# Two transformer blocks in one launch: the head of the program is put in another order, with two later moves

## The reference

```python
mod   = silu(c) @ w_ada + b_ada          # 6 x 1024: sh1, sc1, gt1, sh2, sc2, gt2
mod_c = silu(c_ctx) @ w_ada + b_ada
h  = rmsnorm(x, g_norm1) * (1 + sc1) + sh1
hc = rmsnorm(ctx, g_norm1) * (1 + scc1) + shc1
cq, ckv, kpe, rq, rk, rv, rg = split(h @ w_in)      # the same of hc
q = rmsnorm(cq, g_q) @ w_uq ; k, v from rmsnorm(ckv, g_kv) @ w_ukv
```

## Time and profile before

| | us |
|---|---|
| time, median of 3 (860.28 to 862.14) | 860.43 |
| the profiled execution | 860.81 |
| its span | 858.6 |
| PE busy | 832.7 (97%) |
| weight loads (PEld) busy | 719.3 (84%) |
| DVE busy | 587.7 (68%) |
| ACT busy | 469.6 (55%) |

### The profile page before, as it was taken

The page is one execution under the profiler, slowest core; times in us unless marked ns, Lnnn a source line. Parts: engine busy times, 40 slices in busy tenths (PEclk is TensorE's granted clock), DMA queues, the critical chain, the costliest instruction groups (busy, mean ns, idle before and its releaser), DMA issues. The chain is left out here.

```text
span 858.6 us, 12796 instructions
## 1 busy us (share of the span) xinstructions
PE 832.7 (97%) x4917; PEld 719.3 (84%) x4917; DVE 587.7 (68%) x917; ACT 469.6 (55%) x757; POOL 17.7 (2%) x24
## 2 busy tenths in 40 slices
PE   5999999999999999999999999999999999999997
PEld 4788887867899999987889977788977788888785
DVE  4775968797787778897757677577446655555444
ACT  6686355266456655663456674646535645454442
POOL 1001000000000000000000000010000000000000
PEclk9999999999999999999999999999999999999999
DMA  9964473155656666669758543244605566655551
GB/s 332 355 222 124 148 227 130 50 173 162 205 175 210 181 180 184 178 207 307 240 166 285 175 152 116 75 145 152 194 11 163 171 196 182 186 180 188 185 159 49
DMA packets 103507, 152.85 MB, mean 178 GB/s; under 512 B 6506, under 2 KB 55702, under 8 KB 103448
## 3 DMA queue, kind: packets, MB, share of 16 engines
q1 hardware_dynamic: 102136, 149.15, 55.1%
q10 hardware_dynamic: 1312, 2.90, 1.0%
HBM read 150.97 MB, written 1.05 MB: 177 GB/s over the span
## 5 line engine op out<-in xcount | busy, mean ns | idle before, releaser
L2073 DVE TENSOR_TENSOR w_lo<-raw,w_hi 128x1024 fp32r<-128x1024 f32 (+1 forms) x244 | 294.5, 1212 | 159.1 <-ACT w_hi L1510 158.4
L1510 ACT ACTIVATE w_hi<-raw 128x1024 fp32r<-128x1024 f32 (+1 forms) x244 | 254.8, 1051 | 205.5 <-PE bank L737 141.6
L735 PE MATMUL bank<-w_hi,hT_hi 128*128 128x512 f32 (+2 forms) x400 | 156.0, 390 | 1.8 <-DVE w_lo L2073 1.2
L737 PE MATMUL bank<-w_hi,hT_lo 128*128 128x512 f32 (+2 forms) x400 | 152.9, 382 | 0.0
L736 PE MATMUL bank<-w_lo,hT_hi 128*128 128x512 f32 (+2 forms) x400 | 152.6, 382 | 0.0
L839 PE MATMUL bank<-hT_hi,w_hi 128*128 128x256 f32 x512 | 145.0, 283 | 0.0
L840 PE MATMUL bank<-hT_lo,w_hi 128*128 128x256 f32 x512 | 144.9, 283 | 0.0
L841 PE MATMUL bank<-hT_hi,w_lo 128*128 128x256 f32 x512 | 144.9, 283 | 0.0
L840 PEld LDWEIGHTS bank<-hT_lo,w_hi 128*128 128x128 f32 x512 | 98.3, 192 | 0.0
L841 PEld LDWEIGHTS bank<-hT_hi,w_lo 128*128 128x128 f32 x512 | 98.3, 192 | 0.0
L839 PEld LDWEIGHTS bank<-hT_hi,w_hi 128*128 128x128 f32 x512 | 98.3, 192 | 0.0
(11 more groups left out here) (341 smaller groups left out, 1196.3 us busy)
## 6 DMA issues: line engine op xcount, KB each, us to landing
raw<-w_up_dram SPq DMA_DIRECT2D x132, 256.0 KB, 3.3
raw<-w_ada_dram SPq DMA_DIRECT2D x48, 512.0 KB, 4.7
raw<-w_down_dram SPq DMA_DIRECT2D x44, 512.0 KB, 4.4
raw<-w_in_dram SPq DMA_DIRECT2D x40, 512.0 KB, 4.5
raw<-w_gate_dram SPq DMA_DIRECT2D x44, 256.0 KB, 2.9
raw<-w_out_dram SPq DMA_DIRECT2D x16, 512.0 KB, 3.4
raw<-wk_x_dram SPq DMA_DIRECT2D x8, 512.0 KB, 4.5
raw<-wv_x_dram SPq DMA_DIRECT2D x8, 512.0 KB, 3.4
```

The lines of the kernel that those rows point to most:

```text
L735: pe.matmul(o, xh, yh, start=first, stop=False, skip_group_check=skip)
L737: return pe.matmul(o, xl, yh, start=False, stop=last, skip_group_check=skip)
L1510: act.activation(unit_view(w_hi[n % NSPLIT], u), unit_view(raw[u % NRAW], u), ACT.Copy).then_inc(w_hi_ready, 1)
L2073: dve.tensor_tensor(unit_view(w_lo[n % NSPLIT], u), unit_view(raw[u % NRAW], u), unit_view(w_hi[n % NSPLIT], u).bitcast(F32), ALU.subtract ...
```

## The change

The identity is loaded by SP as its first transfer, and only the two small columns and the ones come on ACT's queue (`in_sel`). `x` comes in two halves with a semaphore each, after units 4 and 6, instead of whole after unit 2; vector groups 2 and 3 and `ctx` are loaded later. ACT does a Silu of one column at once, and rounds no unit before `c_parts`. PE runs 17 fillers ahead of the first chunk, keeps the three fillers only after the first six units, does the spreads earlier or later within the chunks, turns vector group 1 only, and groups 2 and 3 after `rq`. The spread of chunk 3 goes to bank 7 and has eight fillers ahead of its wait instead of eight ahead of `cq`. A unit's pairs of `hT` are awaited one by one, just ahead of the matmul that reads them. The lists of ACT and DVE follow. Two later moves: DVE takes one unit more (a summed one) ahead of the turns of `cq`, `ckv`, `ckvc`, and the subtraction of `wk1`'s last unit goes behind `mix_row`.

```diff
-BUSY = {"score": 8, "ada": 3, "cq": 8, "ffnpre": 14, "gu0": 8}
+BUSY = {"score": 8, "start": 17, "spread": 8, "ada": 3,  "ffnpre": 14, "gu0": 8}
 BY_ROW_TILE = ("wout2_1", "wo1", "dn1")
...
 in_ident = sem("in_ident")
+in_sel = sem("in_sel")
 in_k1 = sem("in_k1")
...
 in_ctxx = sem("in_ctxx")
-in_x = sem("in_x")
+in_x = [sem(f"in_x{t}") for t in range(T)]
 in_gate = sem("in_gate")
...
             first_k = units[u][1]
-            if before is not None:
-                for k in range(first_k, first_k + nk):
-                    before(k)
             pe.wait_ge(unit_ready, u + 1)
...
                     k = first_k + kk
+                    if before is not None:
+                        before(k)
                     ins = step(k, use, hi[:, kk, :], lo[:, kk, :], begin and kk == 0, final and kk == nk - 1)
...
-        emptied(pe, (f"ada{p}", 0))
         use = ("spread", p)
         o = claim(use, next_small() if b is None else b)
+        if p == 3:
+            keep_busy(o[:, P:2 * P], BUSY["spread"])
+        emptied(pe, (f"ada{p}", 0))
         m = modrow[:, p % 2, :]
...
-    pe.wait_ge(c_lo_ready, 2)
     for p in range(4):
         claim((f"ada{p}", 0), p)
+    keep_busy(ps(("ada3", 0))[:, 0:P], BUSY["start"])
+    pe.wait_ge(c_lo_ready, 2)
...
-    for p in range(2):
-        chunk = ada_steps(p)
-        for _ in range(4):
-            chunk_unit(chunk)
-        run(chunk)
-        if p == 0:
-            for g in range(1, len(VEC_GROUPS)):
-                turn_vectors(g)
+    chunk = ada_steps(0)
+    for _ in range(4):
+        chunk_unit(chunk)
+    run(chunk)
+    chunk = ada_steps(1)
+    chunk_unit(chunk)
+    chunk_unit(chunk)
+    turn_vectors(1)
+    next(chunk)
+    pe.wait_ge(in_sel, 16)
     ada_spread(0, 0)
+    run(chunk)
     chunk = ada_steps(2)
-    chunk_unit(chunk)
+    next(chunk)
+    next(chunk)
+    ada_spread(1, 1)
+    next(chunk)
     turn("x1", None, range(2))
-    chunk_unit(chunk)
-    ada_spread(1, 1)
-    chunk_unit(chunk)
-    turn("x1", None, range(2, 4))
     run(chunk)
...
     next(chunk)
+    turn("x1", None, range(2, 4))
     ada_spread(2, 2)
     run(chunk)
-    ada_spread(3, 3)
...
     rq = rows_steps("rq", hT_hi, hT_lo, x1_before, b=2)
+    ada_spread(3, 7)
     next(cq)
...
     run(rq)
+    for g in range(2, len(VEC_GROUPS)):
+        turn_vectors(g)
     rows_panel("ckvpe", hT_hi, hT_lo, turn_before("ctx"), cT, b=4)
...
     count = [0] * NRAW
+    sp.dma_start(ident, const[:, C_ID:C_ID + P]).then_inc(in_ident, 16)
     for u, (name, k0, nk, cols, sources) in enumerate(units):
...
         landed[u] = count[slot]
-        if u == NRAW - 1:
-            for group, done in ((1, in_vec), (2, in_conv), (3, in_conv)):
+        for group, done, at_unit in ((1, in_vec, NRAW - 1), (2, in_conv, first_unit["rq"] + 2),
+                                     (3, in_conv, first_unit["rq"] + 2)):
+            if u == at_unit:
                 for name, _ in VEC_GROUPS[group]:
...
                     sp.dma_start(vrow[g][r:r + n, :], vec_src[name]).then_inc(done, 16)
-        if u == 2:
-            sp.dma_start(res[:, :, :], a["x"].rearrange("(t p) d -> p t d", p=P)).then_inc(in_x, 16)
-        if u == last_unit["ada3"]:
+        for t in range(T):
+            if u == (4, 6)[t]:
+                sp.dma_start(res[:, t, :], a["x"][t * P:(t + 1) * P, :]).then_inc(in_x[t], 16)
+        if u == first_unit["rq"]:
             sp.dma_start(in_ctx[:, :, :], a["ctx"].rearrange("(t p) d -> p t d", p=P)).then_inc(in_ctxx, 16)
...
         act.dma_start(vrow[g][r:r + n, :], vec_src[name]).then_inc(in_c, 16)
-    act.dma_start(k0[:, :], const[:, 0:C_RCOS]).then_inc(in_ident, 16)
+    act.dma_start(k0[:, C_SEL:C_RCOS], const[:, C_SEL:C_RCOS]).then_inc(in_sel, 16)
+    act.wait_ge(mhalf_ready, 1)
+    act.activation(expsink[:, 0:1], mhalf[:, 0:1], ACT.Silu)
...
-    feed_units(2)
     emptied(act, ("vec", 0))
...
-    feed_units(4)
-    act.wait_ge(in_x, 16)
+    feed_units(6)
+    act.wait_ge(in_x[0], 16)
     square("x1", 0, 0, res[:, 0, :])
-    feed_units(6)
-    square("x1", 0, 1, res[:, 1, :])
-    feed_units(7)
     ada(0)
     feed_units(8)
+    act.wait_ge(in_x[1], 16)
+    square("x1", 0, 1, res[:, 1, :])
+    feed_units(10)
     scale_row("x1", res[:, 1, :], row[:, 1, :])
...
     ada(2)
+    feed_units(16)
+    full("x1", 1)
     feed_units(first_unit["cq"] + 1)
-    full("x1", 1)
+    turn("x1", None, [0])
     ada(3)
-    turn("x1", None, range(2))
-    feed_units(first_unit["rq"] + 1)
+    turn("x1", None, [1])
+    feed_units(first_unit["rq"] + 2)
     full("x1", 3)
...
-    feed_units(1)
     columns(0)
...
-    feed_units(6)
+    feed_units(8)
     variance("x1")
-    for g in range(1, len(VEC_GROUPS)):
-        columns(g)
+    columns(1)
+    feed_units(9)
+    scale_rows("x1", [res[:, 0, :]], [row[:, 0, :]])
+    feed_units(10)
     emptied(dve, ("vec", 1))
-    lb = vec("hgrn_lb_2")
-    step(dve.tensor_tensor(lbc[:, 0, :], lb[:, 0:HH], lb[:, HH:2 * HH], ALU.max))
-    settle()
-    for i in range(2):
-        dve.tensor_tensor(lbc[:, 1 + i, :], lb[:, i * HH:(i + 1) * HH], lbc[:, 0, :],
-                          ALU.subtract).then_inc(lb_in_ready, 1)
-    feed_units(7)
-    scale_rows("x1", [res[:, 0, :]], [row[:, 0, :]])
-    feed_units(11)
     spread(0)
-    feed_units(13)
+    feed_units(12)
     spread(1)
...
     turn("ctx", None, range(2, 4))
+    for g in range(2, len(VEC_GROUPS)):
+        columns(g)
+    lb = vec("hgrn_lb_2")
+    step(dve.tensor_tensor(lbc[:, 0, :], lb[:, 0:HH], lb[:, HH:2 * HH], ALU.max))
+    settle()
+    for i in range(2):
+        dve.tensor_tensor(lbc[:, 1 + i, :], lb[:, i * HH:(i + 1) * HH], lbc[:, 0, :],
+                          ALU.subtract).then_inc(lb_in_ready, 1)
...
     feed("rv")
-    feed_units(last_unit["rg"] + 1)
+    feed_units(last_unit["rg"] + 2)
     for name in ("cq", "ckv", "ckvc"):
...
-    feed_units(last_unit["wk1"] + 1)
     dve.wait_ge(rstd_ready, POW["final"] + 1)
...
     dve.tensor_scalar(mix_row[:, 0, :], row[:, 0, :], rs12[:, 0:1], None, ALU.mult).then_inc(row_ready, 1)
+    feed_units(last_unit["wk1"] + 1)
     turn("mix", "wk1")
```

## The result

| | us |
|---|---|
| changed kernel, median of 4 (854.43 to 856.15) | 854.91 |
| kernel before, beside it, median of 4 (860.28 to 862.14) | 861.17 |
| ratio, with its 95% interval | 0.9923 [0.9904, 0.9942] |
| profiled executions, before and after | 860.81, 854.43 |
| their spans | 858.6, 852.6 |

The kernel is faster by 0.77% (0.58 to 0.96). The median beside it, 854.91, is under the forecast too, and only just inside that range. The profiled executions differ by 6.4 us, 6.0 of it within the span.

The account below looks back on a forecast made before the run. TensorE, busy 832.7 of 858.6 us, was taken as the bound. Terms -3.4 - 0.25 + 0.25 + 0.4 - 1.35 = -4.35 from the median 860.43 gave 856.1, stated as 856.2; range 854.6 to 859.2.

Parts of the forecast that it names:

- The move takes nothing from that chain: 0: wk1's subtraction moved behind mix_row: no gain, as DVE's split lay in the shadow of POOL's power; 0, bounds +0.2 and -0.2.
- the dense start: First matmul of the dense run (panel cq): from 40.71 to 37.3 us, -3.4; bounds 36.3 and 39.5.
- the ring of six: Raw slots for DMA, six units back: binds after unit 11 (23.8 us); unit 12 is issued when unit 6 is split.
- That is worth little by itself, for PE isn't what is late next: Start of chunk 0: the fast matmul rate coming at 9.2 us, within unit 0, gains little by itself.
- Third dense unit: PE's wait before 46.98 us, a hole of 0.57: unit rounded ahead, -0.25, between 0 and -0.57.
- ckvpe: Vector groups 2 and 3 pushed behind rq: two transposes +0.25, and a wait for their banks +0.4 (0 to 1.0).
- `rg` + 2: Before uq0: a sum moves into DVE's idle time, so the split starts at 131.9 and PE at 133.05 us; -1.35.
- Rival A: Clock falls once near 23 us and returns 4.7 us later, losing some 2.3 us of work: 858.4; chance 0.11.
- Rival D: Better: no wait at the vectors' banks and dense start at 36.3 us; -5.75, 854.7; chance 0.06.
- B: Slower: clock falls and stays low until the dense run, which starts at 43.9; +2.25, 862.7; chance 0.06.
- C: DMA feed: order only shuffled, later units still depend on ACT; dense start 39.5, -2.15, 858.3; chance 0.12.
- E: w_lo of unit 16 or the change of order gives no gain, within 0.2% of before: 860; chance 0.05.

Follow-up runs that it names:

- best: Changed kernel with vector groups 2 and 3 in banks 0 and 1, plus eight fillers (five after vector group 1, three after unit 7): 853.75 us, ratio 0.9908.
- p_one_plain: Changed kernel with one plain DVE scaling of 1024 elements, result unread, where the subtraction of wk1 stood: 855.14 us, one run.
- b_start_only: Kernel before with only the early identity, early table load, no unit before c_parts and the 17 start fillers: 860.49 us, ratio 1.0001.

## Why the prediction was wrong

The direction, the places and most of the terms were right; the gain was larger than said, at two of its steps.

**The failed step: "The move takes nothing from that chain: 0".** It was -0.74, outside its own bounds of 0.2. I read POOL's 1.91 us as the price of the power, and so saw DVE's subtraction lie in its shadow. But the shadow was made by the subtraction. The trace of before had the hint: the power on 128x8 takes 1.64 us at 164.38 and 2.54 at 561.74. What I left unasked was what POOL's duration would be with DVE idle; the runs with this move alone, with it undone, and with three other instructions in its place put it at 1.01 against 1.91. The Trainium skill (SBUF — State Buffer, Who interferes with whom) says that VectorE and GpSimd share a pair of ports, that the one that starts first holds it for its whole instruction while the other stands still, and that VectorE needs it in its fast copy and scaling mode, and its reading side with two inputs from SBUF. The measurements agree where DVE came first: POOL lost 0.90 us to two inputs, 0.37 to the plain scaling and 0.10 to the first strided one, each the overlap less 0.15. Where POOL came first no run here shows DVE held: the second strided scaling took its 0.42 us beside the power.

**The mis-sized step: the dense start, -3.4 for -4.18.** The forecast's path was the real one, counted slowly. Its own marks beside the trace (DVE's end of a unit): unit 5 15.75 and 15.80, unit 6 18.35 and 18.27, unit 7 20.6 and 20.4, unit 8 22.7 and 22.4, unit 9 24.6 and 24.2, unit 15 34.0 and 33.5. DMA brought the units every 1.35 us, but the first of them sooner than I put it (unit 7 at 18.06 for 18.4, unit 11 at 23.50 for 23.8), and up to unit 15 they kept coming at that pace: the ring of six didn't bind, where I let it bind from unit 12 on. That is 0.5 us at unit 15. The other 0.3 lie behind it: DVE was at the rest of pair 0 at 35.61, I had 36.15, so spread 3 ended at 36.53 without a wait for either. What makes up the 4.2 is told by the undone parts, one profile each: 1.1 for the start, 0.4 for `x`, 0.6 for single pairs. The rest, some 2.1 if the parts simply add, which isn't shown, would be the order of spreads and turns with the leaner list of fillers; of it only the fillers after units 6 to 10 were put back by themselves (0.7). The order of spreads and turns was never undone, so what it is worth stays open.

"That is worth little by itself, for PE isn't what is late next" was right of PE and wrong of ACT. With the start undone ACT is the engine that is late, and hands it on to DMA.

**Third dense unit**: -0.25 predicted, -0.41 measured, within the bounds. **`ckvpe`**: +0.65 predicted, +0.91 measured, within the bounds; the bank wait is 0.57 and ends with the copies, as said. **`rg` + 2**: -1.35 predicted, -1.25 measured between the two places (-1.34 at `uq0` itself), -1.44 alone.

**Rival A** (the clock falls once near 23) happened: half rate from 21.04 to 24.3. I gave it 2.3 us; in this execution it cost nothing that can be seen, for `best` kept the full rate and has the same dense start: ACT and DVE were late there anyhow. In other executions with the same head the low stretch was longer or absent. It was no idle hole that brought it: the longest wait of PE ahead of it was 1.05 us. Rival D's dense start of 36.3 was the nearest to what happened, but its other half, no wait at the banks, did not come true; that its sum of -5.75 lies near the measured -6.03 is luck, for the `mix_row` step isn't in it. B, C and E did not occur: from 24.3 us on the matmuls ran at full rate, and the DMA share was 1.05 from 24 to 31 us.

## What to carry to other kernels

- The duration of an instruction is not its price. If POOL's time for the same shape differs between places, look at what DVE runs beside it. A DVE instruction with two inputs in SBUF, or a scaling at the double rate, that seems free in POOL's shadow may be what casts it; move it behind POOL.
- An early start pays as far as the engine that is late next has room: undo it in the new order before calling it worthless by its worth in the old one, and find its path in the trace, since the same head moved by 0.6 us with the landing of one unit.
- When work is pushed behind into a closed run, look at the bank it takes as well as at its instructions: 0.57 of the 0.91 us were the bank, and another bank gave them back.

## What the runs showed of the hardware

- DVE and POOL: above. POOL's power on 128x4 ended 0.86 to 0.87 us after the end of the DVE instruction that ran when it began, for two inputs in SBUF and for scalings at the double rate. Copies out of PSUM beside it, 1.20 us long, cost the power on 128x8 nothing.
- The clock: of seven profiles whose head before the dense run was the changed kernel's, four had matmuls at half rate between 18.6 and 26 us (a low stretch of 3.4 us in three, 6.8 in one) and three had none. In the kernel before without its fillers after units 6 to 10 the low stretch came at the dense start. It cost between nothing and 1.1 us, by whether PE or another engine was late just there. What decides between the cases is open; PE's load doesn't tell it, for the profile with the least of it from 14 to 24 us (`p_one_plain`, 7.02 of 10) kept the full rate. `b_start_only` had such a stretch at 17 to 20 us, with its fillers in place.
- The table load: ACT's next instruction starts 0.01 us after the load of 1.28 at 2.11. Nothing of the drain of about 1.38 us that the Trainium skill (ScalarE: Activation LUTs, What ACT_TABLE_LOAD costs) puts beside it is to be seen. Nor is it in the kernel before, where ACT had just worked: an instruction up to 7.25, the load at 7.26, the next at 8.56.
- The constants and both `c` vectors were there at 4.33 with the identity in front on SP, against 6.73 behind them on ACT's queue.
